# Turning cached keys on VectorE instead of TensorE in a paged decode stage

## What is computed

```
k_past = cache_k[page_table].reshape(Bd, P, H, hd)      # H = 8 heads of hd = 64
v_past = cache_v[page_table].reshape(Bd, P, H, hd)
s_past = jnp.einsum('bqhd,bkhd->bhqk', q, k_past) * FOX_SCALE
s_past = s_past + c_q - c_past.transpose(0, 2, 1)[:, :, None, :]
...
p = jax.nn.softmax(jnp.concatenate([s_past, s_new], axis=-1), axis=-1)
o = (jnp.einsum('bhqk,bkhd->bqhd', p[..., :P], v_past)
     + jnp.einsum('bhqk,bkhd->bqhd', p[..., P:], v_new))
```

## Time and profile before

| | |
|---|---|
| median of 3 runs | 1650.24 us |
| the profiled execution: its time | 1644.44 us |
| its span, first to last instruction | 1642.8 us |
| busy TensorE (PE) | 1532.9 us, 93% |
| busy VectorE (DVE), ScalarE (ACT) | 671.9 and 603.4 us |
| granted TensorE clock, mean | 0.981 of full |
| data moved | 249.96 MB |
| joined stage | from about 463 to 1322 us |

### The profile page before, as it was taken

One profiled execution on the slowest core, in us unless ns is written; L12 is line 12 of the kernel. 1 busy time (PEld: TensorE's weight loads), 2 busy tenths in 40 slices (PEclk: granted clock), 3 DMA queues, 4 the chain that ended last, 5 costly groups with the idle time before them and its releaser, 6 DMA issues.

```text
span 1642.8 us, 33880 instructions
## 1 busy us (share of the span) xinstructions
PE 1532.9 (93%) x11281; PEld 1262.4 (77%) x11281; DVE 671.9 (41%) x1498; ACT 603.4 (37%) x1287; POOL 501.7 (31%) x952
## 2 busy tenths in 40 slices
PE   5989899998979998999999999999998899999988
PEld 5878787786768776788777887678875688888876
DVE  4444353635434444634445434454354223332221
ACT  5344444444533344324443334533344354111100
POOL 4444434420072134333343333453331123111000
PEclk9999999998989999999999999999999999999999
DMA  4131212122156566776676766777664655222521
GB/s 170 31 84 32 82 44 82 31 63 66 42 168 193 160 196 221 229 221 209 200 235 216 256 205 206 227 236 223 203 205 156 215 214 178 93 94 93 161 90 58
DMA packets 146909, 249.96 MB, mean 152 GB/s; under 512 B 37513, under 2 KB 52362, under 8 KB 146226
## 3 DMA queue, kind: packets, MB, share of 16 engines
q1 hardware_dynamic: 115154, 215.78, 41.8%
q0 software_dynamic: 31584, 32.02, 6.4%
HBM read 217.47 MB, written 30.22 MB: 151 GB/s over the span
## 4 chain that ended last, share of the span: by engine, by line
PE 58%; DMA 4%; ACT 3%; DVE 3%; issue 2%; SPq 1%; POOL 0%; DVEq 0%; ACTq 0%
PE psum L288 24%; PE psum L1895 7%; PE psum L2356 6%; PE psum L1910 4%; PE psum L2348 4%; PE psum L1943 3%; PE psum L2386 3%; DMA w_raw<-in_w_tiles 2%; PE psum L2016 1%; PE psum L2026 1%; DMA v_page<-in_cache_v 1%; PE psum L2023 1%; PE psum L1926 1%; PE psum L1986 1%; PE psum L2395 1%
## 5 line engine op out<-in xcount | busy, mean ns | idle before, releaser
L288 PE MATMUL psum<-h_hi,w_hi 128*128 128x384 f32 (+1 forms) x1344 | 495.3, 368 | 17.9 <-issue 12.9
L288 PE MATMUL psum<-h_hi,w_lo 128*128 128x384 f32 (+1 forms) x1344 | 447.2, 333 | 0.0
L288 PE MATMUL psum<-h_lo,w_hi 128*128 128x384 f32 (+1 forms) x1344 | 446.0, 332 | 0.0
L1465 POOL DMA_DIRECT2D sc<-tmp_bias x512 | 252.6, 502 | 309.0 <-PE psum L1926 306.0
L288 PEld LDWEIGHTS psum<-h_hi,w_hi 128*128 128x128 f32 x1344 | 258.1, 192 | 96.2 <-issue 91.2
L288 PEld LDWEIGHTS psum<-h_lo,w_hi 128*128 128x128 f32 x1344 | 259.3, 193 | 2.4
L288 PEld LDWEIGHTS psum<-h_hi,w_lo 128*128 128x128 f32 x1344 | 257.5, 192 | 0.0
L674 POOL DMA_DIRECT2D lfp<-in_cache_logf x256 | 124.1, 485 | 176.1 <-issue 176.1
L1895 PE MATMUL psum<-con,k_page 128*128 128x128 f32 x1024 | 152.5, 276 | 9.6 <-DVE k_t L1395 6.4
L1514 ACT ACTIVATE k_t<-psum 128x512 f32<-128x512 f32 x128 | 76.1, 595 | 186.9 <-PE psum L1895 186.9
L1895 PEld LDWEIGHTS psum<-con,k_page 128*128 128x128 f32 x1024 | 120.9, 141 | 30.3 <-issue 26.2
(11 more groups left out here) (262 smaller groups left out, 2176.1 us busy)
## 6 DMA issues: line engine op xcount, KB each, us to landing
k_page<-in_cache_k SPq DMA_DIRECT2D x256, 256.0 KB, 3.7
v_page<-in_cache_v SPq DMA_DIRECT2D x256, 256.0 KB, 3.1
w_raw<-in_w_tiles SPq DMA_DIRECT2D x63, 512.0 KB, 4.9
g_pair<-tmp_gates SPq DMA_DIRECT2D x16, 544.0 KB, 4.6
sc<-tmp_bias POOLq DMA_DIRECT2D x512, 16.0 KB, 2.9
tmp_ogla<-gate POOLq DMA_DIRECT2D x4, 1088.0 KB, 5.2
g_pair<-tmp_ogla SPq DMA_DIRECT2D x8, 544.0 KB, 8.0
x_in<-in_x_prompt SPq DMA_DIRECT2D x8, 512.0 KB, 6.1
```

Of the source, the lines that this page charges most:

```text
L288: m = pe.matmul(out, wt[:, s, k, :], h[:, k, t0:t0 + w], start=(k == 0 and a == 0), stop=(k == KT_ - 1 and a == 2))
L1465: pool.dma_start(sc[r0:r0 + TS, j % SLOTS, :], src.to_broadcast([TS, 512])).then_inc(sc_in[j % SLOTS], 16)
```

## The change

- K pages are no longer turned by TensorE. DVE turns each 128x512 page in 32x32 blocks from `k_page` straight to `k_t`, one instruction for a page. In a 32x32 turn, tokens and channels stay inside a strip of 32 partitions, so strip b of `k_t` holds the channels of block f for the tokens of strip b.
- The K load puts token 4i + b on partition 32b + i: its source pattern now runs over 4 (b), then 32 (i), then the row of 512 channels. The target is still 128 partitions by 512.
- Scores are made per eight pages in one step: sixteen 32x32 tiles, token strip tb by head pair hp, into banks 3 to 6 (one for each tb), 128 columns each, in eight rounds (2 halves by 4 channel blocks). The weights come from `q_row`, the queries of each head block repeated in the four strips, made once per sequence by 16 small matmuls (`ql`) and a copy by ACT.
- Banks 3 to 6 are shared with the lifts, the new scores and the V products (columns from 128 on), so waits are added: scores wait until the last lifts are copied and the V sum is gathered; lifts and V steps wait until DVE has read the scores.
- V products accumulate over eight pages, and DVE adds each result to `u_t` (`acc`). All probability lifts are copied by ACT.
- SP loads K page p + 5 when DVE has turned page p.
- The order and the costs: per eight pages `sc`, two turns, `pt`, two turns, `pt`, one turn, `pv`, two turns, `pv`, `acc`, one turn. A K turn has cost 0.3, a score step 2.0.
- `att`, `u_t` and the page table take the place of constants or of spare partitions (space only), and a few waits follow from that.

```
-LIFTED = ("kt", "pt", "pn", "od")
+LIFTED = ("ql", "pt", "pn", "od")
+PAIR = 8
...
+            turns = [(("kt", s, PAIR * j + k), 0.3) for k in range(PAIR)] if has_k else []
+            if has_s:
+                out.append((("sc", p, q), 2.0))
...
+            out += turns[0:2]
...
+                out.append((("pt", x, 2 * g), 0.25))
...
+            out += turns[2:4]
+            if has_x:
+                out.append((("pt", x, 2 * g + 1), 0.25))
...
+            out += turns[4:5]
+            if has_x:
+                out.append((("pv", x, 2 * g), 1.1))
+            out += turns[5:7]
+            if has_x:
+                out.append((("pv", x, 2 * g + 1), 1.1))
...
+                out.append((("acc", x, g), 0))
+            out += turns[7:8]
...
-    decode = [(step, cost * (0.75 if k < first else 1.5 if k > last else 1.0)) for k, (step, cost) in enumerate(decode)]
+    decode = [(step, cost * (0.8 if k < first else 1.2 if k > last else 1.0)) for k, (step, cost) in enumerate(decode)]
...
             def load_k(a):
-                load("cache_k", a // NPG, k_order(a % NPG), k_page[a % NK][:], k_in_page[a % NK])
+                rows = page("cache_k", a // NPG, k_order(a % NPG)).rearrange("o (i b) c -> (o b) i c", b=4)
+                sp.dma_start(k_page[a % NK][:], rows).then_inc(k_in_page[a % NK], 16)
...
             def kstep(s, p):
                 a = s * NPG + p + NK
                 if a < NB * NPG:
-                    wait_lifted(sp, "kt", s, p)
+                    W(sp, "kt_set", s, p + 1)
                     load_k(a)
...
             def kstep(s, p):
-                if copies_it("dve", "kt", s, p):
-                    lift_k(dve, dve.tensor_copy, lift_dve, s, p)
+                a = s * NPG + p
+                dve.wait_ge(k_in_page[a % NK], 16 * (a // NK + 1))
+                W(dve, "sc_mm", 0, a // PAIR)
+                stream.pass_waits(dve)
+                inc(dve.transpose(k_t[:, p // 4 % 2, :, p % 4, :], k_page[a % NK][:].rearrange("p (f c) -> p f c", c=32)), "kt_set")
...
+            def gather(s, g):
+                W(dve, "pv", s, PAIR * (g + 1))
+                part = bank[6][:, P:2 * P]
...
+            def q_turn(s):
+                wait_bank(pe, "ql", s)
+                wait_scores_read(pe, "ql", s)
+                stream.pass_waits(pe)
+                for f in range(4):
+                    for tb in range(4):
+                        m = MM(lift_bank("ql", s)[32 * tb:32 * tb + 32, f * 32:(f + 1) * 32], cc("ident")[:, 32 * f:32 * f + 32],
+                               q_s[:, :, s * TS:(s + 1) * TS], start=True, stop=True)
+                m.then_inc(lifted, 1)
...
+            def sstep(s, j):
+                W(pe, "kt_set", s, PAIR * (j + 1))
...
+                for n in range(max(lifts_before["sc", s, j] - 2, 0), lifts_before["sc", s, j]):
+                    wait_copied(pe, *lift_at[n])
+                pe.wait_ge(S["acc"], 1 + sums_before["sc", s, j])
+                wait_scores_read(pe, "sc", s, j)
+                stream.pass_waits(pe)
+                for half in range(2):
+                    for f in range(4):
+                        for tb in range(4):
+                            rows32 = slice(32 * tb, 32 * tb + 32)
+                            for hp in range(NHP):
+                                c = 24 + 32 * (4 * hp + f) - 16 * half - TS * (f // 2)
+                                m = MM(row_tile(tb, hp), q_row[rows32, c:c + 32], k_t[rows32, half, 4 * hp + f].rearrange("p g t -> p (g t)"),
+                                       start=(half + f == 0), stop=(half == 1 and f == 3))
+                inc(m, "sc_mm")
...
-                        m = MM(bank[6][32 * hp:32 * hp + 32, 0:P], p_t[:, g % 2, col + 32 * hp:col + 32 * hp + 32],
-                               v_page[a % NV][:, hp * P:(hp + 1) * P], start=(x == 0), stop=(x == NPG - 1))
+                        m = MM(bank[6][32 * hp:32 * hp + 32, P:2 * P], p_t[:, g % 2, col + 32 * hp:col + 32 * hp + 32],
+                               v_page[a % NV][:, hp * P:(hp + 1) * P], start=(x % PAIR == 0), stop=(x % PAIR == PAIR - 1))
```

More of the change, by code:

```diff
@@ L1120, in decode_steps @@
     for s in range(STAGES):
[L1121 to L1147, removed]
@@ new lines, in decode_steps @@
+        for j in range(SP):
+            p, q = (s, j - 1) if j else (s - 1, SP - 1)
+            x, g = (s - 1, j - 1) if j else (s - 2, SP - 1)
+            has_k, has_s, has_x = s < NB, 0 <= p < NB, 0 <= x < NB
+            turns = [(("kt", s, PAIR * j + k), 0.3) for k in range(PAIR)] if has_k else []
+            if has_s:
+                out.append((("sc", p, q), 2.0))
+            if j == 0 and has_s:
+                out += [(("new", p), 0.2), (("soft", p), 0), (("exp", p), 0), (("vn_load", p), 0)]
+            out += turns[0:2]
+            if j == 0 and has_k and s:
+                out += [(("qbd", s), 0), (("ql", s), 0.3)]
+            if has_x:
+                out.append((("pt", x, 2 * g), 0.25))
+                if g == 0:
+                    out += [(("sum", x), 0), (("pn", x), 0.1)]
+            out += turns[2:4]
+            if has_x:
+                out.append((("pt", x, 2 * g + 1), 0.25))
+            if s and s * SP + j < NB * SP:
+                out.append((("prep", s * SP + j), 0))
+            out += turns[4:5]
+            if has_x:
+                out.append((("pv", x, 2 * g), 1.1))
+            out += turns[5:7]
+            if has_x:
+                out.append((("pv", x, 2 * g + 1), 1.1))
+                if g == 0:
+                    out.append((("pnv", x), 0.2))
+                out.append((("acc", x, g), 0))
+            out += turns[7:8]
+            if has_x and g == SP - 1:
+                out += [(("out", x), 0), (("od", x), 0.1)]
@@ L1234, in schedule @@
     last = max(k for k, (step, _) in enumerate(decode) if step[0] == "kt")
[L1235 removed]
+    decode = [(step, cost * (0.8 if k < first else 1.2 if k > last else 1.0)) for k, (step, cost) in enumerate(decode)]
     total, work = sum(c for _, c in decode), sum(c for _, c in gla)
[L1237 removed]
+    steps, done, placed = [("prep", j) for j in range(SP)] + [("qbd", 0), ("ql", 0)], LEAD, 0.0
     while placed + gla[0][1] <= done:
@@ L1301, in build_gla @@
         wa_all = shared[NSAMP:NSAMP + RANK].rearrange("p (g c) -> p g c", g=GH)
-        pages = sb(ctx, "pages2", [1, NB * NPG], I32)
-        K_SETS = NPG // 4
+        pages = shared[96:97, 0:NB * NPG].bitcast(I32)
         V_SETS = NPG // 4
@@ L1950, in pn @@
                 wait_bank(pe, "pn", s)
+                wait_scores_read(pe, "pn", s)
                 stream.pass_waits(pe)
```

152 lines of the change are left out of this document (74 added, 78 removed).

## The result

The changed kernel takes 2199.65 us (median of 4 runs, 2194.11 to 2209.63) against 1649.68 us for the kernel before: 1.334 times as long, 95% interval 1.330 to 1.338. The prediction said 1885 us, with a range of 1640 to 2020: the sign was right, the size was not, and the result lies outside the range. The profiled execution has a span of 2194.6 us, 552 us more than before, and all of it lies in the joined stage, which now runs from 463 to about 1874 us: 1411 us in place of 859.

The account below looks back on a forecast made before the run. Before the change PE's in-order queue was the bound; after it, four DMA engines carrying K loads, 1000 us, for a stage taken as 1100 us. 1644.4 - 859 + 1100 = 1885 us, range 1640 to 2020.

Parts of the forecast that it names:

- four engines carry a K load: K page loads: source outermost dimension of 4 means 4 engines with 32 rows each, 3072 fewer packets.
- The sign that K lands late: Changed profile, K loads: landing at 5 us and more in place of 3.7.
- I take 2.3 us: PE, each added score step: 2.3 us, near the V row, 32 x 2.3 = 74 us.
- My upper end of 256 us: PE, all 32 added score steps: 74 us taken, with ends 67 and 256.
- what V waits cost: Paired V steps, with sixteen engines: each pair waits 1.2 to 3 us, 38 to 96 us in 32 pairs.
- one bound for the stage: Joined stage: four DMA engines need 1000 us, more than PE's 754, so they set it; taken as 1100.
- the first case: Four engines carry each K load: 1885 us, own range 1770 to 2020, 78 in 100.
- costs little while data is the bound: PE's granted clock in the stage: lower than 0.99 as PE waits several us at a time, at little cost.
- DVE's turn: DVE, 256 turns of 128x512: 0.69 us each, DVE at 493 us of the stage, covered by PE's queue.
- These cost nothing: DVE and ACT in the stage: 111 us more on DVE, 76 less on ACT, no cost to the time.
- SP's issue of a K load: SP's queue: the same 512 page loads, one issued in 1.11 us.
- sixteen engines, V pairs wait: Rival: loads dealt by target row, PE's 105 us off, 96 us of V waits on; 1635 us, 12 in 100.

Follow-up runs that it names:

- no_loads: The changed kernel with K and V pages loaded once only, without reloads, so results are lost; 1743.64 us.
- sixteen: The changed kernel with K pages read straight through, V rows and bias permuted to fit; 1984.99 us, 1.205 times the kernel before.
- before_k4: The kernel before with one edit, the K load reading its page with an outermost dimension of 4; 1905.6 us.
- all_three: The changed kernel with K loaded over sixteen engines, V steps set apart and score steps cut in two; 1837.7 us, 1.116 times the kernel before.
- apart: The changed kernel, four-engine K load kept, with the two V steps of eight pages set apart in the list; 2023.15 us.

## Why the prediction was right in sign and wrong in size

The 552 us split by stage lengths of three runs: 958 - 859 = 99 us on the engines' side (`no_loads`), 1196 - 958 = 238 us when pages are loaded over 16 engines (`sixteen`), 1411 - 1196 = 215 us for four engines. They add up because each is a difference from the one before. The middle part also holds what V's slower pattern costs in `sixteen`, so it is that much too large and the last that much too small.

**Right: four engines carry a K load.** q1 lost 115154 - 112082 = 3072 packets, 256 x 12, the number that the prediction gave, and a wait with only K and V pages in flight moves 101 GB/s at a share of 0.26. The Trainium skill (DMA: Bandwidth & Descriptors, "Why a DMA increments its semaphore by 16 and not by 1") has the largest count up to 16 that divides both sides, which is 4 here; the trace agrees. In the old order the forecast time comes near as well (`before_k4`, 1905.6 us), with the luck told there. The sign that K lands late could not be read: the record has no landing time for K loads on four engines.

**Wrong: the added score steps, "I take 2.3 us".** The working said that 16 pairs of matmul and weight load cannot need over 0.5 us a round and that all 256 might cost nothing extra. They start 13 ns apart: 256 x 13 ns = 3.3 us, and 3.5 us to the next instruction. A V step's tiles start 109 ns / 4 = 27 ns apart and hid this. On top come the breaks, so 5.8 us at the median, 191 us in 32 steps in place of 74, and 66 us of waits ahead of them. My upper end of 256 us held it; the value taken from the V row did not. The Trainium skill (TensorE: Matmul & The Clock Gate, "Wait — 56ns, not 53.3ns?") has a floor of about 25 ns from the start of one matmul to the next, by which a step would be 6.4 us, an estimate; the trace differs, with 13 ns across sixteen tiles.

**The breaks** were in no step of the prediction. 30 of the 32 score steps have one of over 0.3 us. What speaks for the supply of instructions: they fall at the same matmul of the same step in the changed kernel and in `sixteen` (after the 227th, 177th, 123rd and 251st in the first three steps), whatever the rings do (all 34 of the changed kernel are among the 36 of `sixteen`). Where a step has two, they stand 128 matmuls with 128 weight loads apart. More than that: if all instructions of PE's queue are counted in order (matmuls, weight loads and waits), the breaks of the changed kernel, of `sixteen`, of `no_loads` and of `all_three` all stand a multiple of 256 apart, to within one instruction. q8, the queue of instruction blocks, grew from 93 to 146 packets of 16 KB while the program grew by 2 x (18193 - 11281) = 13824 PE instructions, so about 260 in a packet. In the changed kernel 24 of the 34 breaks have a packet of q8 in flight, and in `sixteen` about nine tenths of the 36; a stretch of 1.9 us picked at random in the same stages has one in about a quarter of cases. Steps half as long cross as many ends of such blocks, 64, and have 12 breaks. So a break belongs to the end of a block of instructions, not to a tile, a bank or a ring. That PE waits there for the next block is inferred from this; no run changed the supply alone.

**Wrong: what V waits cost.** With sixteen engines each pair was to wait "1.2 to 3 us"; it waits 4.2, and what was missing is, as far as the runs show, the issue time of V's new pattern and SP's waits for turns. With four engines the prediction did say that V pages stand behind K pages in the four rings and that PE should wait 5 us and more; it is 335 / 32 = 10.5 us a pair. But these waits stood nowhere in the sum, as if they passed inside the rings' 1100 us.

**Wrong: one bound for the stage.** This is the step that failed most: "K 699, V 174 ... That is 1000 us", stretched by up to 1.23, with all of PE's 754 us beside it at no cost. Rings and PE overlap only as far as five K and four V buffers reach. While PE waits for V, its later results don't come, DVE's turns stand behind them in DVE's queue, and SP's next K loads behind the turns; then the rings run dry while PE works. So the stage became 1.41 times the four rings' 1000 us. In `before_k4`, with V steps evenly spaced, 1.12. That this ring of waits makes the difference is shown as far as `apart` goes: with the same four engines and the V steps spaced it is 1.24. (The "own range 1770 to 2020" of the first case also doesn't follow from its terms: 1026 to 1248 us for the stage gives 1811 to 2033. The result is outside both.)

**Wrong: the clock "costs little while data is the bound".** With the same PE instructions PE was busy for 915.7 us at 0.79 (changed) and 821.6 us at 0.92 (`no_loads`): 94 us more of busy time. How much of it lengthened the stage no run separates.

**Right:** DVE's turn, 694 ns where I took 690, and DVE's busy time in the stage, 449 us where I had 493, never a bound by itself. **Wrong, small:** "These cost nothing", said of DVE's and ACT's work: PE waits 63 us for turns ahead of the score steps in the changed kernel, and 24 us in `no_loads`. And SP's issue of a K load takes 1.87 us and not 1.11.

The rival "sixteen engines, V pairs wait" gave 1635 us for what `sixteen` shows to be 1985: it used the same PE sum, and fell with it.

## What to carry to other kernels

Before moving matmuls into small tiles, count them: the price of the sixteen-tile step here was its number of matmul and weight-load pairs (13 ns each) before it was its columns, and a long run of short ones seems to outrun its instructions. Look at the outermost dimension of both sides of each load; a source of 4 put a page on four engines and cost 215 us or more here, and 258 us in the kernel before. And when two resources feed each other through a few buffers and in-order queues, don't take the larger need as the time: evenly spaced consumers (`apart`: 177 us) were worth nearly as much as twelve more DMA engines.

## What was not expected of the hardware

- At the full granted clock, sixteen 32x32 tiles start a matmul every 13 ns with 128 columns and every 10 ns with 64; the V step, with 128x32 tiles, every 27 ns.
- The time from one page load's issue to the next on SP depends on its pattern: 1.11 us for 128 rows on both sides, 1.31 us for a source of 32 by 4, 1.87 us for one of 4 by 32, and 0.50 us for a further load of 32 rows with the same page number.
- A break, mostly of 1 to 2.5 us, in nearly all runs of 256 short matmuls, with a DMA share of 0.42 or of 0.17, and always at a multiple of 256 instructions of PE's queue from the last one.
- PE's granted clock in the stage was lower the more it stopped: 0.99 before, 0.79, 0.84 and 0.92 in the changed kernel, `sixteen` and `no_loads`; in the 5 us of the wait at 1018 us it was at 0.50, the lower of its levels.
